# Bigger weight pieces, a landing place for row blocks, and a VectorE turn of the inner units in the expert stage of a decoder layer

## The reference, cut to what matters

```
u    = rms_norm(x, norm2_g) * (1 + sc2) + sh2          # 512 x 1024
gate = group-limited top-2 of 16 experts, from softmax(u @ w_router)
for e in range(16):
    h = silu(u @ w1[e]) * (u @ w3[e])                  # w1, w3: 1024 x 512
    y = y + gate[:, e] * (h @ w2[e])                   # w2: 512 x 1024
x = x + g2 * y
```

## Time and profile before

| | us |
|---|---|
| median of 3 runs | 758.55 |
| lowest and highest run | 752.93, 758.62 |
| the profiled execution's own time | 755.66 |
| its span, first to last instruction | 754.0 |

### The profile page before, as it was taken

One profiled execution on the slowest core, in us unless ns is written; L12 is line 12 of the kernel. 1 busy time (PEld: TensorE's weight loads), 2 busy tenths in 40 slices (PEclk: granted clock), 3 DMA queues, 4 the chain that ended last, 5 costly groups with the idle time before them and its releaser, 6 DMA issues.

```text
span 754.0 us, 15645 instructions
## 1 busy us (share of the span) xinstructions
PE 613.6 (81%) x6231; PEld 362.8 (48%) x6235; DVE 322.3 (43%) x925; ACT 255.4 (34%) x611; POOL 80.2 (11%) x119
## 2 busy tenths in 40 slices
PE   0798999977689988799981388999999999999940
PEld 0544474664356666555440254555555555555520
DVE  3713818233279999933336022232232232222215
ACT  3300200113356677822330143433443343344310
POOL 5001000016100000000002200101110110110022
PEclk9998999989779999999995599999999999999985
DMA  8970957061499300056019649999999999999228
GB/s 326 378 306 7 395 212 276 3 204 30 151 335 216 110 1 1 2 207 240 1 48 350 215 167 363 360 372 361 364 375 359 365 375 361 365 366 362 61 60 302
DMA packets 81389, 176.26 MB, mean 234 GB/s; under 512 B 9410, under 2 KB 26378, under 8 KB 79306
## 3 DMA queue, kind: packets, MB, share of 16 engines
q1 hardware_dynamic: 68592, 152.90, 57.9%
q0 software_dynamic: 8384, 13.97, 5.5%
q10 hardware_dynamic: 4380, 8.94, 3.8%
HBM read 155.02 MB, written 20.71 MB: 233 GB/s over the span
## 4 chain that ended last, share of the span: by engine, by line
PE 25%; DMA 24%; issue 3%; DVE 2%; POOL 2%; ACTq 0%; ACT 0%; POOLq 0%
DMA featT<-expert_rows 22%; PE score L1595 9%; PE score L1495 7%; PE bank L1585 4%; PE score L1604 3%; DMA pool_sb<-expert_rows,idx 1%; POOL pool_sb L805 1%; POOL expert_rows L785 1%; DMA expert_rows<-pool_sb,idx 1%; DMA expert_rows<-featT 1%; PE bank L1530 0%; PE bank L1610 0%; ACTq L680 0%; PE bank L1539 0%; PE bank L1550 0%
## 5 line engine op out<-in xcount | busy, mean ns | idle before, releaser
L1595 PE MATMUL score<-pool_sb,featT 128*32 128x256 f32 x2688 | 162.3, 386 | 20.8 <-DMA featT<-expert_rows 12.1
L1595 PEld LDWEIGHTS score<-pool_sb,featT 128*32 128x32 f32 x2688 | 86.7, 111 | 82.4 <-DMA featT<-expert_rows 26.8
L1291 PE MATMUL bank<-pool_sb,featT 128*128 128x512 f32 (+2 forms) x256 | 88.7, 509 | 5.8 <-DVE featT L860 2.6
L1231 DVE TENSOR_TENSOR featT<-featT,score 128x128 f32<-128x128 f32 x42 | 12.1, 288 | 184.7 <-ACT featT L691 184.7
L1604 PE MATMUL score<-pool_sb,featT 128*32 128x256 f32 x1344 | 82.3, 386 | 0.4 <-ACT featT L696 0.4
L1291 PEld LDWEIGHTS bank<-pool_sb,featT 128*128 128x128 f32 x256 | 49.9, 196 | 43.1 <-issue 35.4
L685 ACT ACTIVATE featT<-bank,mod_col 128x32 f32<-128x32 f32 x129 | 39.4, 375 | 61.2 <-PE bank L1585 61.2
L793 POOL DMA_DIRECT2D expert_rows<-featT x42 | 29.2, 695 | 277.8 <-DVE featT L1227 264.0
L1221 DVE TENSOR_SCALAR featT<-bank,mod_col 128x32 f32<-128x32 f32 x215 | 51.0, 304 | 14.9 <-PE bank L1585 14.9
L1495 PE MATMUL score<-pool_sb,featT 128*128 128x512 f32 x128 | 56.9, 597 | 0.0
L691 ACT ACT_TABLE_LOAD x42 | 53.9, 1283 | 0.8
(11 more groups left out here) (255 smaller groups left out, 679.6 us busy)
## 6 DMA issues: line engine op xcount, KB each, us to landing
pool_sb<-in_moe_w SPq DMA_DIRECT2D x48, 2048.0 KB, 22.2
pool_sb<-in_ada_w SPq DMA_DIRECT2D x16, 1024.0 KB, 7.3
expert_rows<-zeros_f SPq DMA_DIRECT2D x17, 512.0 KB, 6.5
featT<-expert_rows ACTq DMA_DIRECT2D x44, 128.0 KB, 5.4
expert_rows<-featT POOLq DMA_DIRECT2D x42, 128.0 KB, 7.0
pool_sb<-in_ada_w SPq DMA_DIRECT2D x8, 640.0 KB, 11.8
pool_sb<-in_w_out SPq DMA_DIRECT2D x4, 1024.0 KB, 16.7
pool_sb<-in_ada_w SPq DMA_DIRECT2D x8, 384.0 KB, 9.7
```

Source lines behind the costliest of these rows:

```text
L1291: m = nc.tensor.matmul(pj_bank(g, i)[:, 0:n], featT[:, k, i * P:(i + 1) * P], w_stage[:, g % 3, k, 0:n], start=(k == 0), stop=(k == KD - 1))
L1595: mm = nc.tensor.matmul(banks[0][h * BT:(h + 1) * BT, 0:2 * HB], xgT[:, k, :], exp_w13[slot][:, :, k, h * HB:(h + 1) * HB], start=(k == 0) ...
```

## The change: what it does

1. **Rows copied to a second place.** The DMA lands in a new place `xg_in` (partitions 32 to 63), and VectorE copies that to `xg` (partitions 0 to 31; `rows_in`, semaphore `m_cp`). ScalarE issues the next load when the copy is done, so three loads ahead of the block in work instead of two. `inner` waits for `m_cp` in place of the landing.
2. **Scale and shift all on VectorE.** The eight transposes land in one bank, and two VectorE instructions over 8 x 32 elements with broadcast operands replace its five and ScalarE's three.
3. **Inner units turned by VectorE.** `hmid` is written with its units in another order (a stride of 32), and one VectorE transpose makes `hT`. PE's `inner_T` and ScalarE's copy go, as does one VectorE-to-PE and one PE-to-ACT semaphore. `inner` has a new wait for `m_h`.
4. **Weight pieces.** w1 and w3 put four consecutive rows on a partition (pieces of 8 KB), w2 four consecutive rows (16 KB). So the features and the inner units must be dealt out in steps of four: the transposes of `xg` and of `x_sb` for the router, eight matmuls of the modulation, `w_router` and `norm2_g` are read with a stride of four elements (`strided`). `norm2_g` goes by 16-byte pieces directly to its columns.
5. **Order.** On VectorE a block is now: product, scale and shift of the next rows, wait for `outer`, turn, `rows_out`, `rows_in`. The load of w1 of expert 2 waits for the scatter instead of the first two row blocks.

```diff
+        xg_in = blkbuf[BT:2 * BT, 0:D]
...
+        def strided(k):
+            at = k // NT * (D // 2) + k % NT
+            return slice(at, (k // NT + 1) * (D // 2), NT)
...
             def load_matrix(e, m):
                 done = e_w2[e % 3] if m == 2 else e_w13[e % 3]
-                sp.dma_start(chunk_of(e % 3, m, DE // P if m == 2 else KD),
-                             MOE_W[m][0, e].rearrange("(k p) n -> p k n", p=P)).then_inc(done, 16)
+                if m == 2:
+                    sp.dma_start(chunk_of(e % 3, m, NT), MOE_W[m][0, e].rearrange("(p k) n -> p k n", p=P)).then_inc(done, 16)
+                else:
+                    sp.dma_start(chunk_of(e % 3, m, KD).rearrange("p (h k) n -> p h k n", h=2),
+                                 MOE_W[m][0, e].rearrange("(h p k) n -> p h k n", h=2, k=NT)).then_inc(done, 16)
...
-            sp.wait_ge(s_xg, 32)
+            sp.wait_ge(s_scat, 16 * 2 * TT)
             load_matrix(2, 0)
...
-            act.dma_start(vrow[16:24, :], norm2_g.rearrange("a (r n) -> (a r) n", n=P)).then_inc(s_small, 16)
+            act.dma_start(vcol[:, 24:32].rearrange("p (h k) -> p h k", h=2), norm2_g[0].rearrange("(h p k) -> p h k", h=2, k=NT)).then_inc(s_small, 16)
...
             def xg_load(g):
-                act.dma_start(xg, xs[bass.ds(g * BT, BT), :]).then_inc(s_xg, 16)
+                act.dma_start(xg_in, xs[bass.ds(g * BT, BT), :]).then_inc(s_xg, 16)
             def block_of_rows(g):
                 act.wait_ge(m_h1, g + 1)
                 nc.scalar.activation(silu, banks[0][:, 0:HB], ACT.Silu).then_inc(m_si, 1)
-                act.wait_ge(m_xt, g + 2)
-                xg_load(g + 2)
-                xg_T(g + 1)
-                act.wait_ge(m_ht, g + 1)
-                nc.scalar.activation(hT, banks[6][:, 0:P], ACT.Copy).then_inc(m_hT, 1)
+                act.wait_ge(m_cp, g + 3)
+                xg_load(g + 3)
...
+            def rows_in(g):
+                dve.wait_ge(s_xg, g * 16 + 16)
+                if not (isinstance(g, int) and g == 0):
+                    dve.wait_ge(m_xt, g)
+                nc.vector.tensor_copy(xg, xg_in).then_inc(m_cp, 1)
             def xg_T(g):
                 dve.wait_ge(m_xt, g + 1)
-                for k in range(5):
-                    m = nc.vector.tensor_scalar(xgT[:, k, :], banks[4][:, k * BT:(k + 1) * BT], mod_col[:, 16 + k:17 + k],
-                                                mod_col[:, 24 + k:25 + k], ALU.mult, ALU.add)
-                m.then_inc(m_xv, 1)
+                nc.vector.tensor_tensor(xgT, banks[4][:, 0:KD * BT].rearrange("p (k r) -> p k r", k=KD),
+                                        mod_col[:, 16:24].unsqueeze(2).broadcast_to([P, KD, BT]), ALU.mult).then_inc(m_sc, 1)
+                dve.wait_ge(m_sc, g + 1)
+                nc.vector.tensor_tensor(xgT, xgT, mod_col[:, 24:32].unsqueeze(2).broadcast_to([P, KD, BT]), ALU.add).then_inc(m_xv, 1)
+            def hmid_T(g):
+                dve.wait_ge(m_h, g + 1)
+                nc.vector.transpose(hT, hmid).then_inc(m_hT, 1)
+            def hidden(g):
                 dve.wait_ge(m_si, g + 1)
-                nc.vector.tensor_tensor(hmid, silu, banks[0][:, HB:2 * HB], ALU.mult).then_inc(m_h, 1)
+                if not (isinstance(g, int) and g == 0):
+                    dve.wait_ge(m_hT, g)
+                nc.vector.tensor_tensor(hmid.rearrange("p (c a) -> p a c", c=NT), silu.rearrange("p (a c) -> p a c", c=NT),
+                                        banks[0][:, HB:2 * HB].rearrange("p (a c) -> p a c", c=NT), ALU.mult).then_inc(m_h, 1)
                 xg_T(g + 1)
+            def block_of_rows(g, y):
+                hidden(g)
+                dve.wait_ge(m_y, g)
+                hmid_T(g)
+                rows_out(y)
+                rows_in(g + 2)
...
             def xg_T():
                 for k in range(KD):
-                    at0 = (k % 5) * BT
-                    m = nc.tensor.transpose(banks[4 + k // 5][:, at0:at0 + BT], xg[:, k * P:(k + 1) * P], ident[0:BT, 0:BT])
+                    m = nc.tensor.transpose(banks[4][:, k * BT:(k + 1) * BT], xg[:, strided(k)], ident[0:BT, 0:BT])
                 m.then_inc(m_xt, 1)
             def inner(slot, g):
-                pe.wait_ge(m_xa, g + 1)
                 pe.wait_ge(m_xv, g + 1)
...
-                        pe.wait_ge(s_xg, g * 16 + 32)
+                        pe.wait_ge(m_cp, g + 2)
...
-            def inner_T(g):
-                pe.wait_ge(m_h, g + 1)
-                nc.tensor.transpose(banks[6][:, 0:P], hmid, ident[:]).then_inc(m_ht, 1)
-
             def stage_of(g, slot, slot_before, uses):
                 pe.wait_ge(e_w13[slot], uses * 32)
+                pe.wait_ge(m_h, g)
                 inner(slot, g)
                 xg_T()
                 pe.wait_ge(e_w2[slot], uses * 16)
                 outer(g - 1, slot_before)
-                inner_T(g)
```

More of the change, by code:

```diff
@@ L339, in decoder_layer @@
         m_xt = sem("m_xt")
-        m_xa = sem("m_xa")
         m_xv = sem("m_xv")
-        m_ht = sem("m_ht")
+        m_cp = sem("m_cp")
+        m_sc = sem("m_sc")
         m_hT = sem("m_hT")
@@ L679, in xg_load @@
             def xg_load(g):
-                act.dma_start(xg, xs[bass.ds(g * BT, BT), :]).then_inc(s_xg, 16)
-            def xg_T(g):
-                for k in range(3):
-                    m = nc.scalar.activation(xgT[:, 5 + k, :], banks[5][:, k * BT:(k + 1) * BT], ACT.Identity,
-                                             scale=mod_col[:, 21 + k:22 + k], bias=mod_col[:, 29 + k:30 + k])
-                m.then_inc(m_xa, 1)
+                act.dma_start(xg_in, xs[bass.ds(g * BT, BT), :]).then_inc(s_xg, 16)
             def block_of_rows(g):
@@ L691, in block_of_rows @@
                 nc.scalar.activation(silu, banks[0][:, 0:HB], ACT.Silu).then_inc(m_si, 1)
-                act.wait_ge(m_xt, g + 2)
-                xg_load(g + 2)
-                xg_T(g + 1)
-                act.wait_ge(m_ht, g + 1)
-                nc.scalar.activation(hT, banks[6][:, 0:P], ACT.Copy).then_inc(m_hT, 1)
+                act.wait_ge(m_cp, g + 3)
+                xg_load(g + 3)
             act.wait_ge(s_scat, 16 * 2 * TT)
             xg_load(0)
-            act.wait_ge(m_xt, 1)
-            xg_load(1)
-            xg_T(0)
+            for g in range(2):
+                act.wait_ge(m_cp, g + 1)
+                xg_load(g + 1)
             act.wait_ge(t_gs, 1)
@@ L1223, in xg_T @@
-                m.then_inc(m_xv, 1)
-            def rows_out(y, upto):
-                dve.wait_ge(m_y, upto)
+                nc.vector.tensor_tensor(xgT, banks[4][:, 0:KD * BT].rearrange("p (k r) -> p k r", k=KD),
+                                        mod_col[:, 16:24].unsqueeze(2).broadcast_to([P, KD, BT]), ALU.mult).then_inc(m_sc, 1)
+                dve.wait_ge(m_sc, g + 1)
+                nc.vector.tensor_tensor(xgT, xgT, mod_col[:, 24:32].unsqueeze(2).broadcast_to([P, KD, BT]), ALU.add).then_inc(m_xv, 1)
@@ L1239, in _ @@
             for g in range(1, 3):
-                block_of_rows(g)
-                rows_out(y_sb[(g - 1) % 2], g)
+                block_of_rows(g, y_sb[(g - 1) % 2])
             with dve.Fori(1, pairs - 1) as m:
-                block_of_rows(m * 2 + 1)
-                dve.wait_ge(s_ys[0], m * 16)
-                rows_out(y_sb[0], m * 2 + 1)
-                block_of_rows(m * 2 + 2)
-                dve.wait_ge(s_ys[1], m * 16)
-                rows_out(y_sb[1], m * 2 + 2)
-            block_of_rows(pairs * 2 - 1)
-            last = dve.value_load(block_start[0:1, NE + 2:NE + 3], min_val=MIN_BLOCKS * NE - 1, max_val=MAXB)
-            rows_out(y_last[0], last)
-            rows_out(y_last[1], last + 1)
+                for n in range(2):
+                    hidden(m * 2 + 1 + n)
+                    dve.wait_ge(m_y, m * 2 + 1 + n)
+                    hmid_T(m * 2 + 1 + n)
+                    dve.wait_ge(s_ys[n], m * 16)
+                    rows_out(y_sb[n])
+                    rows_in(m * 2 + 3 + n)
+            last = dve.value_load(block_start[0:1, NE + 2:NE + 3], min_val=MIN_BLOCKS * NE - 1, max_val=MAXB)
+            hidden(last)
+            dve.wait_ge(m_y, last)
+            hmid_T(last)
+            rows_out(y_last[0])
+            rows_in(last + 2)
+            dve.wait_ge(m_y, last + 1)
+            rows_out(y_last[1])
             for i in range(TT):
@@ L1529, in x2_T @@
                 for k in range(4):
-                    m = nc.tensor.transpose(banks[4 + h][:, k * P:(k + 1) * P], x_sb[:, i, (4 * h + k) * P:(4 * h + k + 1) * P], ident[:])
+                    m = nc.tensor.transpose(banks[4 + h][:, k * P:(k + 1) * P], x_sb[:, i, strided(4 * h + k)], ident[:])
                 m.then_inc(r_tr, 1)
@@ L1624, in expert @@
                     stage_of(g, slot, slot, uses)
-            pe.wait_ge(s_xg, 16)
+            pe.wait_ge(m_cp, 1)
             xg_T()
@@ L1630, in _ @@
             xg_T()
-            inner_T(0)
             pe.wait_ge(t_gs, 1)
```

31 lines of the change are left out of this document (18 added, 13 removed).

## The result

The changed kernel takes 766.83 us (median of 4 runs, 766.07 to 771.35), the kernel before 758.59 beside it: a ratio of 1.0145, 95% interval 1.0111 to 1.0178. It is slower by 1.5%, where 742 was forecast and the range ended at 764.

The account below looks back on a forecast made before the run. The closed loop round one row buffer, about 6.8 us, was taken to bound the kernel. 41 x 6.4 + 3.1 + 1.5 + 3.5 + 0.5 = 271.0 against 288.0, 1 given back: 742 us as a median, range 729 to 764.

Parts of the forecast that it names:

- The loop: Row load issue, landing, VectorE copy, next issue, without PE: a round of 6.4 us against 6.8 before.
- R: Time of one round of the row-load loop: landing 5.4 to 5.5, semaphores about 0.15, copy 0.75, together 6.4 us.
- Row loads land later behind big pieces: Rival, chance 0.15: row-load landings grow beside bigger weight pieces; no gain at 6.05 us, 778 us as a median at 6.5.
- the quiet of 3.4 us: A load on ScalarE's queue beside 8 KB pieces had no packet for 3.4 us, within a 5.3 us landing beside 2 KB.
- The rest: Strided router and modulation reads, 32 transposes and 16 matmuls: 0 to 4 us, taken as 0; late `norm2_g` 0.
- PE: Expert blocks: `inner_T` leaves PE, saving 0.26 us a block, 41 x 0.26 = 10.7; nothing replaces it on PE.
- Strided reads slow the transposes: Rival, chance 0.15: stride adds 0.6 us to each block's eight transposes on PE, 6.82 a block, 754 us.
- The weight pieces: Weight loads in larger pieces: DMA rate up 5%, from 366 to 384 GB/s.
- The start: Before the first block: w1 of expert 2 beside the first row loads costs 0 to 1 us, taken as 0.
- The copy, scale and shift, the turn: VectorE in each block: copy 0.75 us, scale and shift two operations of 0.42, turn 0.28 to 0.56.
- Expert 11's weights: At expert 11 PE reaches 606 us but weights allow 609.6, so they bind for some 3.5 us.
- The sum: Expert stage: 262.4 + 3.1 + 1.5 + 3.5 + 0.5 = 271.0 us against 288.0, 17 less, 1 given back.

## Why the prediction was wrong

- **The loop: the step that failed.** R was "landing 5.4 to 5.5 + 0.15 + 0.75 = 6.4". The form was right (the chain shows load, copy, load), the copy and the semaphores too (0.69 + 0.15). The landing was taken from beside 2 and 4 KB pieces and left as it was. Beside 8 KB pieces it is 5.9, beside 16 KB pieces 6.65, so R is 6.7 to 7.5. Two of the prediction's signs of being wrong came with it: landings over 6, and eight transposes in over a microsecond (1.14). The rival *Row loads land later behind big pieces* named the mechanism and the break-even of 6.05. What I held against it, the quiet of 3.4 us, was true and beside the point: that part stays at 3.5, and the other part, between the row load's own packets, grew by 0.7 and 1.5 us. That part I had named "for it" and then given a small chance.
  The Trainium skill, DMA: Bandwidth & Descriptors, Queues, rings and completion order, lets an engine change from one queue to another only at packet boundaries, some 9 to 17 descriptors apart. The time between a row load's first and last packet grows as that rule would have it. That the first packet waits for a number of descriptors isn't shown, since its 3.4 to 3.7 us are the same beside 2, 4, 8 and 16 KB pieces.
- **The rest: failed.** Strided modulation and router reads were "0 to 4 us, I take 0". They cost the upper end or more: 3.66 us of PE are on the path, and from the modulation to the first row load the strided kernels take 3.7 to 7.2 us more than the packed ones.
- **PE: half right.** `inner_T` gave 0.4 us instead of 0.26 in a block that follows one of its own expert, and nothing at the one change of expert that is undisturbed in both: the period between the last two experts is 6.62 in the kernel before (706.80 to 713.42) and 6.62 in the run with w2 in 4 KB pieces, strided copy and two places (696.84 less 690.22). If the other 14 changes are like it, 26 periods gain 0.41, which is 10.7, as is the forecast's 41 x 0.26: the right sum of two wrong parts, by luck. The strided transposes took 0.46, where the rival *Strided reads slow the transposes* had 0.6. The forecast set this at nothing. The rival's own time, 754, assumed the landing unchanged; the run with w2 in 4 KB pieces has about that, 757.5.
  The Trainium skill, SBUF — State Buffer, on cachelines, says that each access that crosses to a new 16-byte line pays a penalty; PE's 210 against 137 ns and VectorE's 1096 against 682 ns agree with its sign.
- **The weight pieces: right and worthless.** 386 GB/s against a forecast of 384. But in the changed kernel no block waits for weights between 505 and 560: with a slower loop the weights had stopped binding. With the rows out of the loop they bind again, large pieces or not, where PE's block is 5.95; where it is 6.39, with strided transposes, they don't.
- **The start: off.** The load of w1 of expert 2 beside the first row load was forecast at 0 to 1 us, and I took 0; it is 1.9 (7.25 against 5.35 from issue to `inner`).
- **The copy, scale and shift, the turn: right** to 0.07 us.
- **Expert 11's weights: the place right, the size too small.** I had 3.5 us at expert 11. In the small-piece kernels PE waits at experts 10 and 11 for weights and nowhere long for rows. The four blocks of the two take 11.45, 8.05, 9.55 and 8.34 us there, against 7.1, 5.95, 6.6 and 5.95 undisturbed, which is 11.8 more.
- **The sum** has a slip: four changes of expert at 6.85 against 6.4 make 1.8, not 1.5.

In all: the forecast of -16 us became +8 by 19.5 us of pieces and strides. In the periods of the profiled executions the 8 KB pieces cost 5.3, their strides 4.5 and w2 8.1; the rest lies ahead of the first block. Without pieces and strides it is -10 instead of -16, mostly because the wait for weights is 11.8 and not 3.5. What stays open: why the granted clock up to 105 us differs between executions of the same work, whether the strides themselves lower it behind that, and why larger pieces stretch only the second half of a landing.

## What to carry to other kernels

A small transfer in a closed loop is not costed by its own bytes but by the packets of whatever shares the engines; before making other transfers' pieces larger, take the small one out of the loop, here with a second landing place (766.8 to 755.8 us with one edit), and only then ask what the pieces bring. An order of weight rows that suits the DMA is paid for by every engine that must read with its stride, also in stages that look remote: list all such reads, and look for one that another engine waits for. Before single executions are compared, see at one early step that all kernels share whether they were level there. When a wait is moved closer to its user, read from the trace what lies between the release and the user: here 0.41 of 0.57 us was a step that stays, whatever is skipped.

## What the runs showed of the hardware

- A float32 read with a stride of four elements: PE's weight load of a 32-row tile 210 ns instead of 137, 16 loads of 128 rows 3.67 us instead of 1.84, VectorE's copy of 32x1024 1.10 us instead of 0.68.
- VectorE turns 128x128 float32 in 32x32 squares in 0.31 us.
- A 128 KB load's first packet comes, by the medians, 3.4 to 3.7 us after its issue when the engines are full of another queue's packets, whatever their size, and 0.97 us when they are nearly empty; from its first to its last packet 1.2, 1.8 to 1.95 and 2.7 us beside packets of up to 4, 8 and 16 KB.
- The granted clock was 0.57 from 442 to 446 in the changed kernel and 1.00 with w1 of expert 2 late; block 1's 64 matmuls took 5.35 and 3.66 us. Ahead of them PE had stood idle for 0.98 us in both, behind VectorE. No run separates the cause.
- PE waited 4.33 and 4.48 us for weights in two kernels; the 64 matmuls behind took 5.20 and 5.35 us instead of 3.64. Over 594 to 600, around the latter, the granted clock was 0.72, so 1.2 GHz for part of it.
- From the last weight load of `inner` to the first of the transposes 0.41 us pass, with a wait ahead or without.
